# Six late weight pieces loaded in two transfers of 120 and 8 partitions

## What is computed

```python
mod = silu(c) @ ada_w + ada_b                       # shifts, scales and gates
h = rms_norm(x, norm1_g) * (1 + sc1) + sh1
z = h @ w_in                                        # all projections at once
merged = sigmoid(g_nsa) * (o_nsa @ w_br_nsa) + sigmoid(g_dsa) * (o_dsa @ w_br_dsa)
x = x + g1 * (merged @ w_out)
h = rms_norm(x, norm2_g) * (1 + sc2) + sh2
# PEER: 8 heads, each picks 16 of 16384 experts for every token
q = h @ peer_wq                                     # scored against subkeys, two top-16, then top-16 of sums
act = gelu(einsum("cd,chkd->chk", h, peer_u[e]))    # u rows of the chosen experts
out = einsum("chk,chkd->cd", gate * act, peer_v[e]) # v rows of the chosen experts
x = x + g2 * out
y = rms_norm(x, final_g)
```

## Time and profile before

| | |
|---|---|
| median of 3 runs | 935.41 us |
| the three runs | 939.61, 935.41, 935.1 us |
| the profiled execution, whole | 934.36 us |
| its span, first to last instruction | 932.5 us |
| TensorE busy | 777.5 us (83%) |
| VectorE busy | 654.0 us (70%) |
| DMA engines, mean rate over the span | 367 GB/s |

### The profile page before, as it was taken

One profiled execution on the slowest core, in us unless ns is written; L12 is line 12 of the kernel. 1 busy time (PEld: TensorE's weight loads), 2 busy tenths in 40 slices (PEclk: granted clock), 3 DMA queues, 4 the chain that ended last, 5 costly groups with the idle time before them and its releaser, 6 DMA issues.

```text
span 932.5 us, 9676 instructions
## 1 busy us (share of the span) xinstructions
PE 777.5 (83%) x2880; PEld 421.2 (45%) x2880; DVE 654.0 (70%) x1697; ACT 413.6 (44%) x1157; POOL 287.8 (31%) x262
## 2 busy tenths in 40 slices
PE   3999999998988997888777799778687777877785
PEld 2445778888834453454444365323232222222221
DVE  4534679963698978867666867675956757576656
ACT  3112223341468889342334543564634354343433
POOL 0000000000364344542433344525254242533430
PEclk9999999979899999999999999999899999999999
DMA  9967259760599999999999999999999999999993
GB/s 365 422 250 332 91 180 362 280 262 24 230 423 420 423 420 398 423 420 418 418 419 420 420 418 422 420 422 422 419 425 422 420 422 421 420 420 421 421 421 129
DMA packets 47619, 342.33 MB, mean 367 GB/s; under 512 B 5392, under 2 KB 6608, under 8 KB 11088
## 3 DMA queue, kind: packets, MB, share of 16 engines
q0 software_dynamic: 37152, 268.45, 69.4%
q1 hardware_dynamic: 9968, 72.79, 19.5%
q10 hardware_dynamic: 448, 0.48, 0.2%
HBM read 340.65 MB, written 1.05 MB: 366 GB/s over the span
## 4 chain that ended last, share of the span: by engine, by line
DMA 41%; PE 33%; DVE 12%; ACT 6%; issue 3%; POOL 3%; SPq 0%; POOLq 0%; DVEq 0%
DMA extra<-in_uv,arena 22%; DMA arena<-in_uv,arena 15%; PE banks L807 8%; PE banks L562 6%; PE banks L516 5%; PE banks L525 3%; DVE extra L1706 3%; PE banks L777 2%; DMA extra<-in_uv,last_rows 2%; PE banks L747 2%; DVE arena L1706 2%; POOL extra L926 2%; DMA extra<-in_w_ada 2%; PE banks L758 2%; PE banks L676 1%
## 5 line engine op out<-in xcount | busy, mean ns | idle before, releaser
L926 POOL DMA_INDIRECT extra<-in_uv,arena x132 | 148.6, 1125 | 432.2 <-DVE arena L1754 240.5
L807 PE MATMUL banks<-extra 128*128 128x512 f32 x472 | 231.5, 619 | 55.0 <-ACT extra L1164 54.1
L807 PE MATMUL banks<-arena,extra 128*128 128x512 f32 x312 | 154.8, 620 | 39.0 <-ACT extra L1164 38.9
L1151 ACT ACTIVATE arena<-arena 128x1 f32<-128x1 f32 x256 | 51.6, 201 | 303.6 <-DVE arena L1706 303.2
L807 PEld LDWEIGHTS banks<-extra 128*128 128x128 f32 x472 | 82.2, 190 | 180.1 <-ACT extra L1164 110.4
L926 POOL DMA_INDIRECT arena<-in_uv,arena x84 | 95.8, 1140 | 135.0 <-PE banks L807 57.1
L1706 DVE CUSTOM_DVE_ANT_0 extra<-extra 128x1024 f32<-128x1024 f32 x75 | 91.5, 1223 | 35.7 <-DMA extra<-in_uv,arena 34.6
L807 PEld LDWEIGHTS banks<-arena,extra 128*128 128x128 f32 x312 | 54.2, 191 | 128.3 <-ACT extra L1164 83.6
L1706 DVE CUSTOM_DVE_ANT_0 extra<-extra,arena 128x1024 f32<-128x1024 f32 x59 | 72.2, 1225 | 43.5 <-DMA extra<-in_uv,arena 42.9
L1164 ACT ACTIVATE extra<-tab,arena 128x128 f32<-128x128 f32 x234 | 93.9, 401 | 7.7
L807 PE MATMUL banks<-ring,extra 128*128 128x512 f32 x152 | 74.8, 619 | 23.5 <-ACT extra L1164 23.5
(11 more groups left out here) (280 smaller groups left out, 1052.6 us busy)
## 6 DMA issues: line engine op xcount, KB each, us to landing
arena<-in_w_ada SPq DMA_DIRECT2D x6, 2048.0 KB, 8.5
arena<-in_w_late SPq DMA_DIRECT2D x24, 512.0 KB, 8.1
extra<-in_w_ada SPq DMA_DIRECT2D x6, 1024.0 KB, 16.7
extra<-in_w_gate SPq DMA_DIRECT2D x3, 2048.0 KB, 8.0
extra<-in_w_in SPq DMA_DIRECT2D x2, 2048.0 KB, 31.5
extra<-in_w_ada SPq DMA_DIRECT2D x2, 2048.0 KB, 9.8
extra<-in_w_br SPq DMA_DIRECT2D x2, 2048.0 KB, 9.1
arena<-in_w_wq SPq DMA_DIRECT2D x2, 2048.0 KB, 14.5
```

The source lines that it names most:

```text
L807: last = nc.tensor.matmul(acc[tt][:, half * 512:(half + 1) * 512], diag[i % DIAGS], uv_slot[SLOT[v]][:, D + half * 512:D + (half + 1) * 51 ...
L926: nc.gpsimd.indirect_dma_start(uv_slot[SLOT[g]], None, A["uv"], bass.IndirectOffsetOnAxis(ap=expert[:, g:g + 1], axis=0)).then_inc(uv_in[S ...
L1151: link(nc.scalar.activation(gel[:, v:v + 1], dots[:, v:v + 1], ACT.Gelu))
```

## The change

What changes is the load of the pieces with n % 4 = 3, that is 3, 7, 11, 15, 19 and 23, all of them in the fourth buffer. Each is issued as two transfers: partitions 0 to 119, then partitions 120 to 127. Both raise the same semaphore by 16, so `piece` waits for 32 for every load of that buffer. The bytes, the buffers and the order of everything else stay.

```diff
 LATE_NO = {c: n for n, c in enumerate(LATE)}
+NARROW = [n for n, c in enumerate(LATE) if n % 4 == 3]
+NARROW_ROWS = 120
 LSLOTS = 4

             n = LATE_NO[kind, m, j]
-            eng.wait_ge(late_in[n % LSLOTS], 16 * (n // LSLOTS + 1))
+            loads = [1 + (i in NARROW) for i in range(n % LSLOTS, n + 1, LSLOTS)]
+            eng.wait_ge(late_in[n % LSLOTS], 16 * sum(loads))
             return late[n % LSLOTS]

                 if n >= LSLOTS:
                     old, m, j = LATE[n - LSLOTS]
                     sp.wait_ge(...)
+                if n in NARROW:
+                    sp.dma_start(late[n % LSLOTS][0:NARROW_ROWS, :], A["w_late"][n][0:NARROW_ROWS, :]).then_inc(late_in[n % LSLOTS], 16)
+                    sp.dma_start(late[n % LSLOTS][NARROW_ROWS:P, :], A["w_late"][n][NARROW_ROWS:P, :]).then_inc(late_in[n % LSLOTS], 16)
+                    continue
                 sp.dma_start(late[n % LSLOTS], A["w_late"][n]).then_inc(late_in[n % LSLOTS], 16)
```

## The result

| | before | after |
|---|---|---|
| median | 935.40 us | **948.54 us** |
| runs | 935.1 to 939.61 (4) | 947.54 to 950.19 (4) |
| ratio | | 1.0146, 95% interval 1.0111 to 1.0181 |
| span of the profiled execution | 932.5 us | 945.5 us |

The change costs 13.1 us by the medians, or 2.2 us for each of the six pieces (10.4 to 16.9 us by the interval). The forecast was 3.6 us of gain, with a range up to 937.0. Where a loss of an experiment is given in us beside its ratio, it is worked out from the ratio.

What follows compares the result with a forecast made beforehand. The prediction took the DMA engines to bound the kernel, with one ending 4.5 us late. Sparing that engine gave 3.6 us of gain, all other terms 0, so 935.41 became 931.8 us, range 930.2 to 937.0.

Steps and rivals of the forecast that it cites:

- What bounds the kernel: From the first late piece to the last gather, the bytes moved by the DMA engines set the pace.
- The split over the engines: In the six cut pieces, 120 partitions go to engines 0 to 14 and 8 to engines 0 to 7.
- SyncE's issues: Six more issues of 0.33 us, 2.0 us in all, covered by SyncE's waits for TensorE: 0.
- the arrival of the pieces: The wait ends at the later part; a ninth row ends a piece 0.16 us later: 0.
- the constants: TensorE's constants in its waits change nothing: 0.
- The engine left out is the straggler: The engine spared 7.5 us is the one ending 4.5 us behind the second: gain 3.6 us, chance 0.50.
- The tail of one engine alone: In the drain at the end, ten slices of 0.45 us with one engine should shrink to five to seven.
- a loss of 0.9 us: Rival: the engine ending last is among eight with a ninth row; 0.93 us lost, 936.3 us, chance 0.15.
- A row takes 4096 bytes / 26.3 GB/s = 0.156 us: Row time in the six pieces: the engine left out is spared 7.5 us, eight others get 0.93 us more.
- nothing changes: Rival: even spread, an ordinary engine left out, or time tied to where rows land; 935.4 us, chance 0.27.
- the eight rows on one engine: Rival: the engine ending last carries all eight rows, +7.5 us; chance 0.08, shared with other losses over 4.7 us.

Runs made afterwards that it cites:

- the gate block: Late pieces whole, gate blocks and subkeys cut at 64 or at 120 instead, against the kernel before: 936.89 and 934.17 us in one run each.

## Why the prediction was wrong

**What bounds the kernel: right.** The DMA engines did set the pace, and it was by their rate that the 13.1 us were lost.

**The split over the engines: right.** 15 and 8 engines, by the count of 42 packets. The Trainium skill's rule, page "DMA: Bandwidth & Descriptors", section "Why a DMA increments its semaphore by 16 and not by 1", that the largest number up to 16 that divides the partitions is taken, holds here. Which engines they are no run shows.

**SyncE's issues, the arrival of the pieces, the constants: right, 0.** The column cut with its two transfers a piece is equal to before within its interval, and TensorE's list has no wait for a piece.

**The engine left out is the straggler: wrong.** This was a judgement without a row, and the forecast hung on it. The tail of one engine alone is ten slices (4.5 us) in the kernel after, and with 60 rows it was as long as with 64, though one engine was spared 15 us. So by the prediction's own sum the change would have been worth nothing or a loss of 0.9 us even had every row kept its price.

**"A row takes 4096 bytes / 26.3 GB/s = 0.156 us": the step that failed.** The sum gave every row the same price whoever carried it and wherever it went. That holds for a whole transfer of 128 partitions and roughly for 32 to 95, and not for 0 to 119. The reading that fits all runs is that an engine that writes into partitions which another one serves slows both: around piece 11 the rate was 337 GB/s instead of 420 with all engines busy. The price is 2.2 us a piece. Together with the missing gain of 3.6 us this is the whole distance of 16.7 us to the forecast.

The thought was in the text, in the rival "nothing changes": the straggler's time may belong to the place where its rows land. But it was priced at no gain. The worked case stopped at the one engine that mattered for the forecast, and never asked what the rows do to the 15 others if places count: each of the others then writes into a foreign place as well. That would have been the slower rival, with an estimate from rows: eight rows of 0.156 us that are served twice over in six pieces, 7.5 us, where 13.1 were found. The slower rival that stood in its stead, the eight rows on one engine at 942.9 us, has no run behind it, and the count of packets speaks against it.

The Trainium skill's remark "don't bother", page "DMA: Bandwidth & Descriptors", section "Rules for kernel authors", which the prediction set against the change, was right in its advice. The prediction took it as a reason for no change, and here two halves of 64 partitions cost 10.3 us for six pieces. What fits the runs is another part of the Trainium skill, which the prediction had passed over, page "DMA: Bandwidth & Descriptors", section "The descriptor swizzle": in a transfer of 128 partitions engine 0 has partitions 0 to 3 and 32 to 35, engine 1 has 4 to 7 and 36 to 39, and so on, with 64 to 127 for engines 8 to 15. By it, a transfer into 32 to 95 that gives four rows to each engine in order puts each one exactly in its own place, one into 36 to 95 puts each in its neighbour's, and one into 0 to 63 puts two in each of eight places. The runs agree in this order: 922.6 (64 rows; 923.4 with 60), 937.9 and 943.5 us. That this assignment is the reason is inferred from the times; no record here names an engine. A simpler reading is that only the rows which land in a place count, whoever brings them. With this assignment 0 to 63 would put eight rows into each of eight places, as a whole piece does into all, and would be at 936 us: that could be some 14 of the 21 us between 0 to 63 and 32 to 95, and not the rest. And it would make 36 to 95 as fast as 32 to 91, four rows to a place in both, where 14 us were found. So it matters who brings them.

Open is which engine the straggler is, and what part of the 2.2 us of a piece comes from engines of the same transfer and what part from the gathers. Both happen: the gate block shows the first with no gather near, the move by four partitions the second. Rounds that take twice as long in the gate block are what one would see if a place took in no more than one engine's rate; that is an estimate, not shown.

## What to carry to other kernels

Where the DMA engines are the bound, load with all 128 partitions in one transfer, and cut along the columns if it has to be cut: two transfers of 128 partitions cost nothing here, where two of 64, of 96 and 32, or of 120 and 8 cost 1.4 to 2.2 us for 512 KB beside gathers. If only part of the partitions is wanted, where they begin counts as much as how many they are. And a busy share tells half of the story: set the rate beside it, for DMA engines at a share of 1.02 moved anything from 337 to 420 GB/s.

## What the runs showed of the hardware

- Four partitions decide. 60 rows into 32 to 91 leave the rate from 420 to 480 us at 420 GB/s, and 60 rows into 36 to 95 bring it down to 373 and cost some 14 us over 24 pieces; the source rows are without effect (922.55 and 936.32 us crossed).
- A load cut by partitions is slow even alone: 2 MB took 6.3 us whole, 9.3 us as 64 and 64 and 10.5 us as 120 and 8 partitions, so 333, 226 and 200 GB/s with nothing but one packet beside it.
- The number of engines of a transfer can be read from the page, if each adds one small packet, as the counts fit throughout: 128, 96, 64 and 32 partitions took 16 engines, 120 and 60 took 15 and 8 took 8.
- One engine ends alone behind the others, by 4.5 us before and after, and by 3.6 us with 64 and with 60 rows, though one engine was spared 15 us in the last.
